# Modulation in blocks of 256 shift and 256 scale columns, and the first two input segments built up by pairs of contraction blocks

## The reference

```python
mod = silu(c) @ w_mod[l] + b_mod[l]                 # 1024 -> 6*1024, for both streams
sh1, sc1, g1, sh2, sc2, g2 = split(mod, 6)
h = rmsnorm(x, norm1_g) * (1 + sc1) + sh1           # 384 x 1024
z = h @ w_in[l]                                     # 1024 -> 5024: u, q, k, v, latents, three gates
...                                                 # pooling, window attention, latent attention
x = x + g1 * y
h = rmsnorm(x, norm2_g) * (1 + sc2) + sh2
x = x + g2 * mixture_of_experts(h)                  # 16 experts, 1024 -> 1024 -> 1024
```

## Time and profile before

| | |
|---|---|
| median of 3 runs | 1780.69 us (1779.1 to 1782.38) |
| profiled execution | 1780.58 us, its span 1778.5 us |
| TensorE matmul busy | 1697.8 us, 95% of the span |
| TensorE weight load, DVE, ACT, POOL busy | 800.8, 648.1, 289.9, 118.6 us |
| moved by DMA | 533.81 MB, mean 300 GB/s |
| layer 0 mixing, from the first matmul to the first expert matmul | 10.2 to 451 us |
| layer 1 mixing begins | 895 us |

### The profile page before, as it was taken

How to read it: one execution, slowest core, us unless ns; L and a number is a source line. 1 busy time by engine, 2 the same in 40 slices (tenths; PEclk the granted TensorE clock), 3 DMA queues, 4 the chain that set the end, 5 groups by cost and what they waited for, 6 DMA issues and landing times.

```text
span 1778.5 us, 18819 instructions
## 1 busy us (share of the span) xinstructions
PE 1697.8 (95%) x7152; PEld 800.8 (45%) x7152; DVE 648.1 (36%) x1375; ACT 289.9 (16%) x735; POOL 118.6 (7%) x161
## 2 busy tenths in 40 slices
PE   7999999999999998898999999999999998988988
PEld 3466566654434332242345565666553432323322
DVE  1257555566122120121124566565661211201211
ACT  2234222012101010000022432221030100000100
POOL 0251000000000000000012500000000000000000
PEclk9999999999999999999999999999999999999999
DMA  9531233765999999999983223238559999999997
GB/s 396 186 116 48 107 119 119 279 236 198 411 429 428 428 428 429 428 428 428 426 348 139 101 82 115 105 116 330 224 212 413 428 428 429 429 428 428 429 428 327
DMA packets 49250, 533.81 MB, mean 300 GB/s; under 512 B 5856, under 2 KB 7040, under 8 KB 10528
## 3 DMA queue, kind: packets, MB, share of 16 engines
q1 hardware_dynamic: 45360, 522.74, 71.3%
q0 software_dynamic: 2112, 7.97, 1.3%
q10 hardware_dynamic: 1712, 2.20, 0.4%
HBM read 530.76 MB, written 2.13 MB: 300 GB/s over the span
## 4 chain that ended last, share of the span: by engine, by line
PE 74%; DMA 22%; DVE 2%; issue 1%; ACT 1%; SPq 0%; POOL 0%; DVEq 0%
PE bank L2081 21%; DMA ring<-in_w_moe 21%; PE bank L1682 12%; PE bank L1701 7%; PE bank L1748 6%; PE bank L2118 5%; PE bank L1930 5%; PE bank L1784 2%; DMA ring<-in_w_mix 2%; PE bank L1844 2%; PE bank L1997 1%; PE bank L1710 1%; PE bank L1819 1%; PE bank L1673 1%; PE bank L1670 1%; PE bank L1868 1%
## 5 line engine op out<-in xcount | busy, mean ns | idle before, releaser
L1682 PE MATMUL bank<-hT,ring 128*128 128x384 f32 x768 | 258.2, 489 | 0.0
L2081 PE MATMUL bank<-M,hT 128*64 128x512 f32 x992 | 221.4, 595 | 16.6 <-DMA M<-in_w_moe 16.1
L2081 PE MATMUL bank<-ring,hT 128*64 128x512 f32 x1024 | 227.1, 594 | 9.9 <-DMA ring<-in_w_moe 9.9
L1682 PEld LDWEIGHTS bank<-hT,ring 128*128 128x128 f32 x768 | 143.6, 190 | 102.5 <-issue 6.7
L2081 PEld LDWEIGHTS bank<-ring,hT 128*64 128x64 f32 x1024 | 72.5, 137 | 156.0 <-issue 139.8
L2081 PEld LDWEIGHTS bank<-M,hT 128*64 128x64 f32 x992 | 69.9, 137 | 158.1 <-issue 133.9
L1701 PE MATMUL bank<-M,ring 128*128 128x384 f32 x384 | 136.1, 498 | 0.7 <-ACT M L792 0.7
L2081 PE MATMUL bank<-ring,M 128*64 128x512 f32 x512 | 115.4, 596 | 15.5 <-DMA ring<-in_w_moe 14.2
L2081 PE MATMUL bank<-M 128*64 128x512 f32 x512 | 115.9, 595 | 14.4 <-DMA M<-in_w_moe 14.4
L1748 PE MATMUL bank<-ring,hT 128*128 128x512 f32 (+1 forms) x288 | 117.6, 568 | 0.5 <-DVE hT L1113 0.3
L989 ACT ACTIVATE hT<-bank 128x512 f32<-128x512 f32 x32 | 19.1, 598 | 571.9 <-PE bank L2081 571.9
(11 more groups left out here) (243 smaller groups left out, 1537.8 us busy)
## 6 DMA issues: line engine op xcount, KB each, us to landing
ring<-in_w_moe SPq DMA_DIRECT2D x96, 2048.0 KB, 30.7
M<-in_w_moe SPq DMA_DIRECT2D x94, 2048.0 KB, 30.4
ring<-in_w_mix SPq DMA_DIRECT2D x110, 1024.0 KB, 5.2
arena<-in_w_moe SPq DMA_DIRECT2D x2, 2048.0 KB, 14.7
ring<-in_w_mix SPq DMA_DIRECT2D x4, 576.0 KB, 5.0
arena<-in_bias_rows POOLq DMA_DIRECT2D x4, 512.0 KB, 6.5
g2slot<-in_bias_rows POOLq DMA_DIRECT2D x4, 512.0 KB, 7.3
M<-in_counts POOLq DMA_DIRECT2D x2, 768.0 KB, 8.1
```

The source lines that it names most:

```text
L1682: ins = mm(ps[:, 0:TOK], w[:, q, (j % 4) * P:(j % 4 + 1) * P], hT[:, 4 * h + q, :], start=(h == 0 and q == 0), stop=(h == 1 and q == 3))
L2081: ins = mm(bank[b][64 * e:64 * e + 64, :], lhs(e, 4 * h + q), w[:, q, :], start=(h == 0 and q == 0), stop=(h == 1 and q == 3))
```

## The change

Shift and scale are taken in blocks of 256 channels. The host packs ("mod", q) for q = 0 to 3 as 256 shift columns beside the matching 256 scale columns, so one modulation block gives everything for two contraction blocks, kb = 2q and 2q + 1. FRONT, BACK, h_raw and h_scale are gone. For each pair q TensorE does mod(q), two tiles of segment 1 for pair q - 1, the columns of q, the six transposes of the pair, the third tile of segment 1, and segment 0 for pair q. Each block is scaled out of its bank, the even one by DVE, the odd one by ACT. In layer 1 ACT copies mod 0 ahead of its sums of squares; before, DVE did it after the first tile's xn. The banks: mod 0 in 0, its columns in 3; for q > 0 mod in 6, columns in 7; transposes of the pair in 6 and 7. UNITS and ISSUE are reordered to match.

```diff
@@ plan_banks
-    for k, i in enumerate((0, 2)):
-        use(("mod", i), k)
-    use(("modcol", 0), 2)
-    for kb in (FRONT + BACK if l else BACK + FRONT):
-        use(("h1", kb), 4 + kb % 4)
...
+    use(("mod", 0), 0)
+    use(("modcol", 0), 3)
+    for q in range(NQ):
+        if q:
+            use(("mod", q), 6)
+            use(("modcol", q), 7)
+        for k in range(2):
+            use(("h1", 2 * q + k), 6 + k)
+        if q == 0:
+            for j in range(2):
+                for t in range(T):
+                    use(("seg", j, t), 3 * j + t)
@@ plan_units and ISSUE
-    units += [("mod", 1, 1), ("mod", 0, 0), ("mod", 0, 1), ("mod", 2, 0), ("mod", 2, 1), ("seg", 0, 0), ("mod", 1, 0),
-              ("mod", 3, 0), ("seg", 1, 1), ("mod", 3, 1), ("seg", 1, 0), ("seg", 0, 1)]
+    units += [("mod", 2, 1), ("mod", 0, 0), ("mod", 0, 1), ("mod", 1, 0), ("mod", 1, 1), ("seg", 0, 0), ("mod", 2, 0),
+              ("seg", 1, 0), ("seg", 1, 1), ("seg", 0, 1), ("mod", 3, 0), ("mod", 3, 1)]
-ISSUE = [1, 2, 3, 4, 5, 6, 0, 7, 9, 10, 11, 8] + list(range(12, NU - 4)) + [NU - 1, NU - 2, NU - 4, NU - 3]
+ISSUE = [1, 2, 5, 3, 4, 7, 6, 0, 9, 10, 11, 8] + list(range(12, NU - 4)) + [NU - 1, NU - 2, NU - 4, NU - 3]
@@ ACT
             for l in range(L):
+                if l > 0:
+                    mod_row(l, 0)
                 x_stats(l, 0)
                 if l == 0:
                     mod_row(l, 0)
...
+                for q in range(NQ):
+                    if q:
+                        mod_row(l, q)
+                    h_evac(l, q)
@@ DVE
+            def h_evac(l, q):
+                kb = 2 * q
                 ps = wait_full(dve, l, ("h1", kb))
...
+                V.tensor_scalar(hT[:, kb, 0:P], ps[:, 0:P], amp[0][:, kb, 0:1], shift[0][:, kb, 0:1], ALU.mult, ALU.add)\
+                    .then_inc(front_dve, 1)
...
-                if l > 0:
-                    mod_row(l, 0)
                 first_variance(2)
                 normalise(1)
                 normalise(2)
...
+                for q in range(NQ):
+                    mod_cols(l, 0, q, 2 * q, 2 * q + 2, q + 1)
+                    h_evac(l, q)
@@ PE
-                mod(l, 2)
-                begin(l, ("modcol", 0))
-                mod_cols(l, 0, 0, 0, False)
-                mod_cols(l, 0, 2, 1, True)
-                norm_turn(l, "h1", 0, FRONT)
                 segment(0, 0, range(T))
...
+                for q in range(1, NQ):
+                    mod(l, q)
+                    segment(1, q - 1, (0, 1))
+                    mod_cols(l, q)
+                    norm_turn(l, q)
+                    segment(1, q - 1, (2,))
+                    segment(0, q, range(T))
+                segment(1, NQ - 1, range(T))
+                for q in range(NQ):
+                    segment(2, q, range(T))
@@ mixing_units
+            if i < NQ:
+                w = np.concatenate([v["w_mod"][:, half, c + i * 256:c + (i + 1) * 256] for c in (0, D)], axis=2)
```

More of the change, by code:

```diff
@@ L104, in count_table @@
     return out.reshape(1, 4 * TOK)
-FRONT, BACK = tuple(range(KB // 2)), tuple(range(KB // 2, KB))
-MODROW = {0: 0, 2: 1, 1: 0, 3: 1}
+NQ = KB // 2
 TILES = (1, 2, 0)
@@ L645, in _ @@
                 if l == 0:
-                    pool.wait_ge(landed[slot_of(UNITS[5])], 16)
+                    pool.wait_ge(*unit_landing(l, ("seg", 1, 0)))
                 pool.dma_start(rows[:, :], a["rows"][l].partition_broadcast(P)).then_inc(rows_in, 16)
@@ L749, in mod_row @@
                 read(l, ("mod", i), F(row_of(i), ps[:, :], ACT.Copy))
[L751 to L762, removed]
-                ps = wait_full(act, l, ("h1", kb))
[L764 to L771, removed]
+            def h_evac(l, q):
+                act.wait_ge(cols_ready, NQ * l + q + 1)
+                kb = 2 * q + 1
+                ps = wait_full(act, l, ("h1", kb))
+                F(hT[:, kb, 0:P], ps[:, 0:P], ACT.Identity, scale=amp[0][:, kb, 0:1], bias=shift[0][:, kb, 0:1])\
+                    .then_inc(front_act, 1)
+                act.wait_ge(front_act, NQ * l + q + 1)
+                read(l, ("h1", kb), F(hT[:, kb, P:TOK], ps[:, P:TOK], ACT.Identity, scale=amp[0][:, kb, 1:2],
+                                      bias=shift[0][:, kb, 1:2]))
             def exps(l, m, j):
@@ L1097, in mod_cols, with h_evac @@
                 V.tensor_tensor(amp[k][:, lo:hi, :], amp[k][:, lo:hi, :], col(g0), ALU.mult).then_inc(cols_ready, 1)
-                dve.wait_ge(cols_ready, 2 * l + count)
-            def h_raw(l, kb):
+                dve.wait_ge(cols_ready, NQ * l + count)
+            def h_evac(l, q):
+                kb = 2 * q
                 ps = wait_full(dve, l, ("h1", kb))
[L1102 to L1119, removed]
+                V.tensor_scalar(hT[:, kb, 0:P], ps[:, 0:P], amp[0][:, kb, 0:1], shift[0][:, kb, 0:1], ALU.mult, ALU.add)\
+                    .then_inc(front_dve, 1)
+                dve.wait_ge(front_dve, NQ * l + q + 1)
+                read(l, ("h1", kb), V.tensor_scalar(hT[:, kb, P:TOK], ps[:, P:TOK], amp[0][:, kb, 1:2], shift[0][:, kb, 1:2],
+                                                    ALU.mult, ALU.add))
             def merge(l, b, j):
@@ L1636, in mod, with mod_cols, norm_turn @@
                         done(l, ("mod", i), ins)
-            def mod_cols(l, k, i, j, last):
+            def mod_cols(l, i):
                 wait_read(pe, l, ("mod", i))
-                ps = bank[turn(l, ("modcol", k))[0]]
+                ps = begin(l, ("modcol", i))
                 for c in range(4):
[L1643 to L1648, removed]
+                    ins = mm(ps[:, 2 * c:2 * c + 2], row_of(i)[:, c * P:(c + 1) * P], pair, start=True, stop=True)
+                done(l, ("modcol", i), ins)
+            def norm_turn(l, q):
                 for t in range(T):
                     pe.wait_ge(xn_ready, 3 * l + t + 1)
-                    for kb in kbs:
-                        ps = begin(l, (name, kb)) if t == 0 else bank[turn(l, (name, kb))[0]]
+                    for kb in (2 * q, 2 * q + 1):
+                        ps = begin(l, ("h1", kb)) if t == 0 else bank[turn(l, ("h1", kb))[0]]
                         ins = turn_over(ps[:, t * P:(t + 1) * P], xn[:, t, kb * P:(kb + 1) * P], ident)
                         if t == T - 1:
-                            done(l, (name, kb), ins)
+                            done(l, ("h1", kb), ins)
             def scores(l, m):
```

83 lines of the change are left out of this document (19 added, 64 removed).

## The result

The changed kernel is slower: 1791.78 us median of 6 runs (1786.95 to 1794.08) against 1780.59 us for the kernel before (1779.10 to 1782.75, 6 runs), ratio 1.0059 with a 95% interval of 1.0046 to 1.0072. The medians are 11.2 us apart, where 5.9 us was forecast with a range up to 1789.8 us. The direction was right and the size was not: the time lies above the range.

What follows compares the result with a forecast made beforehand. It took TensorE to bound the mixing part of a layer and the weight stream the expert part. Layer 0 +0.9, bank waits +1.8 and layer 1 +3.2 gave 5.9 us slower, 1786.5 us, range 1781.8 to 1789.8.

Steps and rivals of the forecast that it cites:

- layer 0: segment 0 starts earlier: Layer 0 mixing: segment 0 starts at about 18.4 us instead of 22.33, 3.9 us earlier.
- layer 0: deferred mod, columns, transposes: Layer 0: one modulation block, four column matmuls and 18 transposes now come after 22.33 us, +4.94 us.
- layer 0: small wait that goes: Layer 0 mixing: of TensorE's small waits, 0.17 us goes.
- layer 0: first segment group at half speed: Layer 0, first segment matmuls: the sum took the clock as held at full speed, no cost.
- bank 7, three times a layer: Pairs 1 to 3: transposes wait 0.6 us for DVE to read shift and scale, +1.8 us in each layer.
- layer 1: earlier start, counted from mod 0: Layer 1: segment 0 starts at 900.6 us instead of 902.95, 2.35 us earlier.
- layer 1: deferred work, wait that goes: Layer 1: modulation block, columns and six transposes add 3.48 us; the 0.92 us wait at 915.90 goes.
- layer 1: clock: Layer 1: 2.7 us of segment work falls in the half-speed dip, losing 1.35 instead of 0.2 us, +1.15.
- by the row: Layer 0: transposes kept the clock up from 18.68 to 22.33 us in the trace, against the Trainium skill's rule.
- The first rival: Layer 0: the clock falls there too, a 3.4 us dip at half speed, +1.7 us: 1788.2 us, chance 0.27.
- The second rival: Bank wait only 0.1 us and layer 1's dip misses the segment: 2.2 us in all, 1782.8 us, chance 0.2.
- the third (deferred work absorbed): New waits and idle time between segment matmuls absorb the 8.4 us deferred: -3.7 us, 1776.9 us, chance 0.07.

Runs made afterwards that it cites:

- experiments 2: Changed kernel with the column matmuls of pairs 1 to 3 one tile earlier, between the first and second tile of segment 1: 1788.52 us.
- experiment 6: Changed kernel with four extra 128x256 matmuls on TensorE while it waits for the first weights: 1792.31 us.
- 8: Changed kernel with 22 extra 128x128 transposes behind the column matmuls of layer 1 alone: 1788.47 us.
- experiment 11: Changed kernel with modulation block 1 before the first segment group, columns of pairs 1 to 3 one tile earlier, one 128x384 matmul in each layer's attention: 1779.87 us.
- experiment 7: Kernel before with four extra 128x256 matmuls on TensorE while it waits for the first weights: 1781.58 us, ratio 1.0003.
- experiment 9: Kernel before with one extra 128x384 matmul in each layer's attention, ahead of block 6's column matmuls: 1780.47 us, ratio 0.9996.

## Why the prediction was wrong in size

The working added up term by term, and each term can be held against the traces.

| term | forecast | measured |
|---|---|---|
| layer 0: segment 0 starts earlier | -3.9 | -2.6 (19.72 against 22.33) |
| layer 0: deferred mod, columns, transposes | +4.9 | +4.9 taken over |
| layer 0: small wait that goes | -0.2 | -0.2 |
| layer 0: first segment group at half speed | 0 | +3.1 (8.40 against 5.27) |
| bank 7, three times a layer | +1.8 | +1.56 |
| layer 1: earlier start, counted from mod 0 | -2.35 | -2.24 (10.68 against 12.92) |
| layer 1: deferred work, wait that goes | +2.6 | +2.6 taken over |
| layer 1: clock | +1.15 | +2.8 (8.21 against 5.27, less 0.18 of before) |

The measured column gives 6.8 us for layer 0 (milestone 7.0) and 4.7 us for layer 1 (milestone 4.9).

Right: the deferred work is not hidden; the waits on bank 7 come three times a layer, ended by the amp operation, at 0.52 us instead of 0.6; layer 1's segment starts within 0.1 us of the place forecast; no mixing weight ends a TensorE wait after 20 us; the rest of a layer only shifts.

Wrong: **the price of the clock**, in two steps. In layer 0 the sum went "by the row", that the clock held between 18.68 and 22.33, and put a dip at 0.27 and 1.7 us. But that stretch had twelve transposes back to back behind a modulation block; the new one has six with gaps, and TensorE never left half speed from 10.2 to 25.8 us in the changed kernel. All four traces of kernels that keep this start of layer 0 without a filler (the changed kernel, experiments 2, 6 and 8) have a group of 7.2 to 8.4 us, so the slow group is no matter of one execution. The moment of the rise is not fixed, though: in experiment 11, with the same instructions on TensorE up to the columns, the clock was up by then. It cost 3.1 us in the group and, of the 1.3 us by which the segment was late, 0.8 us in the columns; another 0.3 us was x, which landed later in this execution. In layer 1 I moved the interval of the earlier trace rows as it stood, and let the clock rise 2.7 us into the segment. The rise, though, came 5.7 us after the segment's start, for the half-speed time began only 1.1 us ahead of the segment and lasted 6.8 us instead of 3.4. That size is in part the execution's: in experiment 6 the fall came 3.9 us ahead of the segment, the group took 6.82 us, and 1.55 us were lost, close to the 1.35 us of the working. The first rival had the mechanism for layer 0 right, and its price less than half. With 3.9 us in layer 0 in place of 0 and 2.8 in place of 1.15 us in layer 1, the same sum gives 11.4 us, or 10.9 us with the bank wait as measured. The medians differ by 11.2 us, the two stretches of the profiled executions by 11.9 us.

The second rival (a small bank wait, a harmless dip) and the third (deferred work absorbed) are excluded by the same rows. What stays open: what decides when the clock falls and rises. In layer 1 all three traces of the changed start without filler (the changed kernel, experiments 2 and 6) have 6.8 us at half speed, but so has one of three of the kernel before's start (experiment 7), and the other two have 3.4 us. Against that execution the changed kernel's layer 1 is 3.2 us longer, not 4.9. The traces show only what ran in each.

## What to carry to other kernels

When a serial stretch at the start of a stage is shortened by taking work out of it, that work was also what kept TensorE's clock up; price the first matmuls behind the gap at half speed for several microseconds (5.7 and 6.1 us here), not for the length of one dip seen elsewhere. Split work so that something ready always stands between a producer chain on DVE and the matmuls that need it: moving one modulation block there took 9.3 us off the median, while the profile notes 1.26 us of idle time before the segment of layer 0 and 3.45 us (1.85, 0.39, 0.75 and 0.46) in layer 1. Where two short-lived results share a bank, put a tile of other work between the last write of the one and the first write of the other.

## What was unexpected in the hardware

A useless matmul in an idle gap can pay. Three of them in 1.9 us of idle time shortened the next group from 8.21 to 5.39 us, and 22 transposes did as much.

Behind a gap as short as 0.66 us and the one-column matmuls that follow it, the clock fell in 11 of 20 passes; with a single 128x384 matmul in the gap it fell in 0 of 6. The times alone don't confirm it: experiment 9 was not faster than the kernel before. So some of the 4 us between the runs of one kernel is the clock's doing: the program up to the segment was the same in three executions of the kernel before and its variants, and TensorE's mod 2 took 2.02, 2.63 and 2.57 us.

Starting TensorE early did not help: in the changed kernel a clock that had risen by 10.3 us was down again after 1.66 us of waiting, and in the kernel before, where it stayed up over 1.51 us of waiting, the time was the same.
